# Moving the root-mean-square sums and their spread into the second weight group of two gated layers

## The chip, the core and the metric

The kernel runs on one core of a Trainium2 chip. The metric is the device time of one execution in microseconds (us), as the median of several runs. In the trace the engines are PE (TensorE, matmuls), PEld (its weight loads), DVE (VectorE), ACT (ScalarE), POOL (GpSimd) and SP (the queue that issues the loads of the weights).

## The reference, cut to what matters

Two model blocks follow one another on a sequence of 512 tokens of 1024 channels. The change touches two layers of the first block, its two gated feed-forward layers behind a root mean square (here f1 and f2):

```python
def rms_norm(x, g):
    xf = x.astype(jnp.float32)
    y = xf * lax.rsqrt(jnp.mean(xf * xf, axis=-1, keepdims=True) + NORM_EPS)
    return (y * g.astype(jnp.float32)).astype(x.dtype)

def swiglu(x, w_in, w_out):
    gate, up = jnp.split(x @ w_in, 2, axis=-1)
    return (jax.nn.silu(gate) * up) @ w_out

h = rms_norm(x, ffn1_pre_g[l])
x = x + 0.5 * rms_norm(swiglu(h, ffn1_w_in[l], ffn1_w_out[l]), ffn1_post_g[l])
```

w_in is 1024 x 5632, that is 22 tiles of 128 gate channels and 22 of up channels. The factor of the root mean square is one number per token, so it can be multiplied in behind the matmul: the gates are multiplied by it before silu and once more after silu, for the ups. Between f1 and f2 stands a mixer of attention and a state space; the second block has four more gated layers (a0, b0, a1, b1), which have a layer norm and are not touched.

## The kernel before

**Layout.** Activations are held transposed, channels on 128 partitions and the 512 tokens along the free dimension: X, and its halves Hh and Hl (a high part that the fast float format holds, and the rest). Each weight is split in the same way into whi and wlo. A product of a tile is then three matmuls of 128 x 512: hi by hi, lo by hi and hi by lo (L325 to L327, or L339, L340 and L345 where a group opens).

**Weights.** They come in units of eight 128 x 128 tiles, 512 KB each, in the order of use, and there are four slots (NS = 4). SP loads a unit once PE is done with the unit four before it. ACT copies it to whi (L792, `hi`), then DVE subtracts to get wlo (L1283, `lo`), then PE may use it. Both engines do this in program order, at most two units ahead of the tile that they stand at (AHEAD = 2, `hi_to` and `lo_to`).

**The gated layer, `ffn`.** A group is one pair of gates and the two ups that belong to it: four PSUM banks are filled by eight steps k over the input channels, 4 tiles and 12 matmuls a step, 96 in all, from four units of weights. There are 11 groups (j = 0, 2, ..., 20). I call them group 1, 2, 3 and so on, and number the layer's units from 0: group 1 uses units 0 to 3, group 2 units 4 to 7, group 3 starts with unit 8. While PE works on one group, the other engines work on the one before it, in this chain: DVE multiplies gate 0 and gate 1 by Rb (L1331, "gate in"), which empties their banks; ACT takes silu of each (L853); POOL multiplies each by Rb again (L2022); DVE multiplies by the ups (L1338), which empties the other two banks; ACT copies the product to Ah (L867) and DVE subtracts for Al (L1345). PE has eight banks, taken in turn, four of them held by the running group.

**The root mean square.** The squares are summed over channels by POOL and ACT into acc and sq. PE sums these over partitions by small matmuls (`rms_cols`, L431 and L436) beside step k = 6 of group 1; ACT takes the root (L814), DVE the reciprocal (L1305) and splits it (colr); PE spreads it over all partitions (`spread`, L446) at the end of group 1; ACT copies it to Rb (L828). So sums and spread take the banks 5 and 6 of the turn, and group 2 takes 7, 8, 1 and 2. Its third and fourth bank are those of the two gates of group 1.

**Side work.** In f1 ACT and DVE also advance a generator `s5_small`, which prepares tables for the mixer in small pieces: one piece at steps k = 2 and 5 of each group but the first, and one at the end of each pair. On ACT the pieces use Exp (L961, L964) and later Sin. Every switch between Sqrt, Exp, Silu and Sin costs an ACT_TABLE_LOAD.

Of the kernel before, what the change touches and what calls it, by code (L numbers as in the profile page):

```python
# [5 lines left out]
P = 128  # L6
T = 512
D = 1024
KD = D // P
# [171 lines left out]
def build(nc, x_d, w_d, cst_d, s5_d, att_d, msk_d, out_d):  # L181
# [52 lines left out]
        assert offset + size <= 229344, (name, offset + size)  # L234
        return nc.alloc_sbuf_tensor_at(name, list(shape), dt, offset=offset), offset

    Ah, _ = ar("Ah", [P, NF, T], F32R)
    Al, _ = ar("Al", [P, NF, T], F32R)
    Y, _ = ar("Y", [P, KD, T], F32)
    cur[0] = arena  # L240
    Qf, _ = ar("Qf", [P, 4, T], F32)
    Kf, _ = ar("Kf", [P, 4, T], F32)
# [59 lines left out]
    def tensor_program(pe):  # L302
# [153 lines left out]
                    last = name == "sq" and p_ == (1 if perm else 0)  # L456
                    col_sums(src[:, :], b, 8 * p_, (("full", (tag, "cols")),) if last else (), p_ == 1)

        def rms_mid(st, perm=False):
            def mid(k):  # L460
                if k == KD - 2:
                    rms_cols(st, perm)
                if k == KD - 1:
                    spread(0, (st, "rms"), ("spread", st))
            return mid

        def ffn(st, rms):
            for j in range(0, NF, 2):
                gemm_group((st, j), st if j == 0 else None, (("H free", st),) if j == NF - 2 else (),
                           rms_mid(st) if rms and j == 0 else None)  # L470

        def bank_squares(st, k):

# [307 lines left out]
    def scalar_program(act):  # L781
# [35 lines left out]
        def rms_mid(st, k, n=4):  # L817
            if k == KD - 2:
# [3 lines left out]
            if k == KD - 1:  # L822
# [11 lines left out]
                act.activation(X[:, k, :], X[:, k, :], ACT.Copy, scale=ALPHA).then_inc(  # L834
                    *S.done("scales", ("X scaled", st, k)))

        def ffn(st, rms, arena_free, side=None, tmp_free=()):
            for j in range(0, NF, 2):
                p = START[st] + j // 2 * 4 * KD
                for k in range(KD):  # L840
                    hi_to(p + 4 * k + 3)
                    if side and j and k in (2, 5):
                        next(side, None)
                    if j == 0 and rms:
                        rms_mid(st, k)
                if j == 2 and not rms:
                    scale_x(st)
                if not rms:
                    act.wait_ge(*S.at(("full", (st, j))))
                for i in range(2):  # L850
                    if rms:
                        act.wait_ge(*S.at(("gate in", st, j + i)))
                        act.activation(tmp[i][:, :], tmp[i][:, :], ACT.Silu).then_inc(  # L853
                            *S.done("silu", ("silu", st, j + i)))
                    else:
                        if j:
                            act.wait_ge(*S.at(("product", st, j - 2 + i)))
                        else:
                            act.wait_ge(*S.at(tmp_free + (i,)))
                        act.activation(tmp[i][:, :], bank(((st, j), i))[:, :], ACT.Silu).then_inc(  # L860
                            *S.done("silu", ("silu", st, j + i), empties=[((st, j), i)]))
                if j == 0:
                    for key in arena_free:
                        act.wait_ge(*S.at(key))
                for i in range(2):
                    act.wait_ge(*S.at(("product", st, j + i)))
                    act.activation(Ah[:, j + i, :], tmp[2 + i][:, :], ACT.Copy).then_inc(  # L867
                        *S.done("moving_hi", ("Ah", st, j + i)))
                if side:
                    next(side, None)  # L870

        def square(st, k, src):

# [376 lines left out]
            if k == 1:  # L1250
                hi(1)
        side = s5_small()
        ffn("f1", True, (), side)
# [3 lines left out]
        ffn("f2", True, (("Hl", "m1o", 7), ("full", ("glu", 3))))  # L1257
# [12 lines left out]
    def vector_program(dve):  # L1270
# [42 lines left out]
        def ffn(st, rms, arena_free, side=None):  # L1313
            for j in range(0, NF, 2):
                p = START[st] + j // 2 * 4 * KD
                for k in range(KD):
                    lo_to(p + 4 * k + 3)
                    if side and j and k in (2, 5):
                        next(side, None)
                    if rms and j == 0 and k == KD - 2:  # L1320
                        rms_recip(st, (st, "rms"))
                gate = [bank(((st, j), i))[:, :] for i in range(2)]
                up = [bank(((st, j), 2 + i))[:, :] for i in range(2)]
                dve.wait_ge(*S.at(("full", (st, j))))
                if rms:
                    if j == 0:
                        dve.wait_ge(*S.at(("Rb", st)))
                    for i in range(2):
                        if j:
                            dve.wait_ge(*S.at(("product", st, j - 2 + i)))  # L1330
                        dve.tensor_tensor(tmp[i][:, :], gate[i], Rb[:, :], MUL).then_inc(  # L1331
                            *S.done("gates", ("gate in", st, j + i), empties=[((st, j), i)]))
                for i in range(2):
                    dve.wait_ge(*S.at(("gate" if rms else "silu", st, j + i)))
                    if j:
                        dve.wait_ge(*S.at(("Al", st, j - 2 + i)))
                    keys = (("product", st, j + i),) + ((("last product", st, i),) if j == NF - 2 else ())
                    dve.tensor_tensor(tmp[2 + i][:, :], up[i], tmp[i][:, :], MUL).then_inc(  # L1338
                        *S.done("gates", *keys, empties=[((st, j), 2 + i)]))
                if j == 0:  # L1340
                    for key in arena_free:
                        dve.wait_ge(*S.at(key))
                for i in range(2):
                    dve.wait_ge(*S.at(("Ah", st, j + i)))
                    dve.tensor_tensor(Al[:, j + i, :], tmp[2 + i][:, :], f32(Ah[:, j + i, :]), SUB).then_inc(  # L1345
                        *S.done("moving_lo", ("Al", st, j + i)))
                if side:
                    next(side, None)

        def add_square(st, k, tag):  # L1350
            dve.wait_ge(*S.at(("square", st, k)))
# [622 lines left out]
            if k == 1:  # L1974
                lo(1)
        side = s5_small()
        ffn("f1", True, (), side)
# [4 lines left out]
        ffn("f2", True, (("full", ("glu", 3)),))  # L1982
# [365 lines left out]
```

## Time and profile before

| | us |
|---|---|
| median of 3 runs | 3035.84 (3031.92 to 3036.48) |
| the profiled execution's own time | 3040.53 |
| its span in the trace | 3038.7 |
| PE busy | 2953.3, 97% of the span |
| DVE busy | 1327.3, 44% |
| ACT busy | 1002.3, 33% |
| POOL busy | 403.4, 13% |
| weights, share of the 16 DMA engines | 26.4% |

Of the chain of work that ended last 93% is PE, 4% DVE, and 1% ACT. A busy share of PE counts matmuls by modelled ends that overlap their successors, so what the rows tell is the start of each matmul: at the full clock of 2.4 GHz one 128 x 512 matmul starts every 0.227 us, at 1.2 GHz every 0.43 us. Idle time in square brackets names what ended it.

### The profile page before, as it was taken

How to read it: one execution, taken by the hardware profiler on the slowest of the kernel's cores; microseconds unless marked ns; L12 is line 12 of the kernel's file. 1: busy time of each engine (PE TensorE's matmuls, PEld its weight loads, DVE VectorE, ACT ScalarE, POOL GpSimd, SP SyncE). 2: the span in 40 equal slices, each digit the busy share in tenths (PEclk: the TensorE clock that was granted, in tenths of full speed). 3: DMA queues.
4: the chain of work that ended last, by engine and by line, in shares of the span. 5: the costliest groups of instructions: out<-in, count | busy, mean ns of one | idle time of the engine just before them, and what ended most of it. 6: DMA issues, size and time to landing. Idle time of an engine off the chain costs nothing.

```text
span 3038.7 us, 32142 instructions
## 1 busy us (share of the span) xinstructions
PE 2953.3 (97%) x13432; PEld 2434.2 (80%) x13432; DVE 1327.3 (44%) x1783; ACT 1002.3 (33%) x1345; POOL 403.4 (13%) x427
## 2 busy tenths in 40 slices
PE   8999989899999999999999999999999999899998
PEld 6888876577888788888887888888888788788887
DVE  5553267645343433334655333343333465543333
ACT  4232234453232333223333332233222333342222
POOL 3110057312110000011231000100001123200010
PEclk9999989899999999999998999999999899899998
DMA  4333212122233232232212222222333221122222
GB/s 137 96 97 97 97 56 69 17 72 88 97 97 97 85 97 97 97 96 77 77 49 64 97 97 97 97 77 97 97 97 96 72 76 49 63 97 97 96 91 77
DMA packets 76016, 260.39 MB, mean 86 GB/s; under 512 B 11728, under 2 KB 11856, under 8 KB 75856
## 3 DMA queue, kind: packets, MB, share of 16 engines
q1 hardware_dynamic: 75872, 258.34, 26.4%
q8 instruction: 106, 1.74, 0.2%
q14 instruction: 38, 0.31, 0.0%
HBM read 255.03 MB, written 2.10 MB: 85 GB/s over the span
## 4 chain that ended last, share of the span: by engine, by line
PE 93%; DVE 4%; issue 1%; ACT 1%; POOL 0%; DMA 0%; SPq 0%; DVEq 0%; POOLq 0%; ACTq 0%
PE bank L325 25%; PE bank L327 25%; PE bank L326 25%; PE bank L339 2%; PE bank L340 2%; PE bank L345 2%; PE bank L436 2%; PE bank L683 2%; PE bank L446 1%; DVE Hl L1291 1%; PE bank L374 1%; PE bank L375 1%; PE bank L378 1%; PE bank L590 1%; PE bank L608 1%
## 5 line engine op out<-in xcount | busy, mean ns | idle before, releaser
L1283 DVE TENSOR_TENSOR wlo<-wraw,whi 128x1024 fp32r<-128x1024 f32 x474 | 588.1, 1253 | 832.4 <-ACT whi L792 831.7
L325 PE MATMUL bank<-Hh,whi 128*128 128x512 f32 x2320 | 911.5, 393 | 11.0 <-DVE wlo L1283 9.1
L326 PE MATMUL bank<-Hh,wlo 128*128 128x512 f32 x2320 | 906.5, 391 | 0.0
L327 PE MATMUL bank<-Hl,whi 128*128 128x512 f32 x2320 | 906.1, 391 | 0.0
L792 ACT ACTIVATE whi<-wraw 128x1024 fp32r<-128x1024 f32 x479 | 498.9, 1055 | 957.8 <-DMA wraw<-weights 957.5
L325 PEld LDWEIGHTS bank<-Hh,whi 128*128 128x128 f32 x2320 | 438.3, 189 | 106.4 <-issue 11.7
L327 PEld LDWEIGHTS bank<-Hl,whi 128*128 128x128 f32 x2320 | 437.8, 189 | 92.4
L326 PEld LDWEIGHTS bank<-Hh,wlo 128*128 128x128 f32 x2320 | 437.9, 189 | 89.3
L325 PE MATMUL bank<-Ah,whi 128*128 128x512 f32 x1056 | 411.8, 390 | 0.0
L326 PE MATMUL bank<-Ah,wlo 128*128 128x512 f32 x1056 | 410.9, 389 | 0.0
L327 PE MATMUL bank<-Al,whi 128*128 128x512 f32 x1056 | 410.8, 389 | 0.0
L327 PEld LDWEIGHTS bank<-Al,whi 128*128 128x128 f32 x1056 | 198.2, 188 | 41.3
L326 PEld LDWEIGHTS bank<-Ah,wlo 128*128 128x128 f32 x1056 | 198.3, 188 | 40.8
L325 PEld LDWEIGHTS bank<-Ah,whi 128*128 128x128 f32 x1056 | 198.3, 188 | 40.6
L1338 DVE TENSOR_TENSOR tmp<-bank,tmp 128x512 f32<-128x512 f32 x132 | 87.2, 688 | 239.6 <-ACT tmp L860 193.9
L2028 POOL TENSOR_TENSOR zsum<-Y 128x512 f32<-128x512 f32 x6 | 10.4, 1730 | 1220.6 <-DVE Y L1417 1220.6
L339 PE MATMUL bank<-Hh,whi 128*128 128x512 f32 x304 | 128.6, 423 | 24.0 <-issue 8.4
L340 PE MATMUL bank<-Hh,wlo 128*128 128x512 f32 x304 | 125.8, 414 | 0.0
L860 ACT ACTIVATE tmp<-bank 128x512 f32<-128x512 f32 x88 | 47.8, 595 | 197.3 <-PE bank L327 197.3
L2022 POOL TENSOR_TENSOR tmp<-tmp,Rb 128x512 f32<-128x512 f32 x44 | 56.0, 1295 | 413.3 <-ACT tmp L853 413.3
L867 ACT ACTIVATE Ah<-tmp 128x512 fp32r<-128x512 f32 x132 | 81.7, 632 | 62.2 <-DVE tmp L1338 62.2
L339 PEld LDWEIGHTS bank<-Hh,whi 128*128 128x128 f32 x304 | 61.3, 202 | 40.7 <-issue 18.6
(258 smaller groups left out, 2528.1 us busy)
## 6 DMA issues: line engine op xcount, KB each, us to landing
wraw<-weights SPq DMA_DIRECT2D x479, 512.0 KB, 3.4
X<-x_t SPq DMA_DIRECT2D x8, 256.0 KB, 6.9
y_t<-X SPq DMA_DIRECT2D x8, 256.0 KB, 2.0
Y<-masks SPq DMA_DIRECT2D x1, 512.0 KB, 8.5
MUb<-ssm SPq DMA_DIRECT2D x1, 256.0 KB, 7.9
tmp<-ssm SPq DMA_DIRECT2D x1, 256.0 KB, 3.9
zsum<-attention SPq DMA_DIRECT2D x1, 256.0 KB, 4.0
MUb<-attention SPq DMA_DIRECT2D x1, 256.0 KB, 4.2
```

The costliest lines, as they stand in the source:

```text
L325: pe.matmul(b, sh, mh, start=start, stop=False)
L326: pe.matmul(b, sl, mh, start=False, stop=False)
L327: signal(pe.matmul(b, sh, ml, start=False, stop=stop), keys)
L339: pe.matmul(bs[i][:, :], hi, Hh[:, 0, :], start=True, stop=False)
L340: pe.matmul(bs[i][:, :], lo, Hh[:, 0, :], start=False, stop=False)
L345: signal(pe.matmul(bs[i][:, :], hi, Hl[:, 0, :], start=False, stop=False), ends)
L436: ins = pe.matmul(b[:, col + 2 * m:col + 2 * m + 2], lhsT, ones[:, 0:2], start=False, stop=m == 3, skip_group_check=True)
L683: ins = pe.matmul(b[:, s], KS[:, h, s], QP[:, h, s], start=True, stop=True, skip_group_check=True)
L792: act.activation(whi[:, u % NS, :], wraw[:, u % NS, :], ACT.Copy).then_inc(*S.done("weights_hi", ("hi", u)))
L867: act.activation(Ah[:, j + i, :], tmp[2 + i][:, :], ACT.Copy).then_inc(*S.done("moving_hi", ("Ah", st, j + i)))
L1283: dve.tensor_tensor(wlo[:, u % NS, :], wraw[:, u % NS, :], f32(whi[:, u % NS, :]), SUB).then_inc(*S.done("weights_lo", ("lo", u)))
L1338: dve.tensor_tensor(tmp[2 + i][:, :], up[i], tmp[i][:, :], MUL).then_inc(*S.done("gates", *keys, empties=[((st, j), 2 + i)]))
```

## The change

In f1 and f2 alone (a new argument `late`):

- The column sums of PE move from step 6 of group 1 to step 2 of group 2, and the spread from the end of group 1 to the end of step 4 of group 2. Root, reciprocal and the copy to Rb move along.
- Group 1 is copied out of its four banks by ACT (`aside`, four copies of 128 x 512) into raw4, which lies over the last four tiles of Ah. The gates and ups of group 1 are then read from raw4.
- The whole pair of group 1 (`pair(0)`: gate in, silu, POOL's product, product, Ah, Al) runs on ACT and DVE at step 5 of group 2, ahead of the split of unit 9, which is done at step 6.
- The banks: group 1 takes 1 to 4, group 2 takes 5 to 8, sums and spread 1 and 2, and group 3 takes 3, 4, 5 and 6. Its third and fourth bank are those of the two gates of group 2.

```diff
+    raw4, _ = ar("raw4", [P, 4, T], F32, o_ah + (NF - 4) * T * 4)
 # PE
-                           rms_mid(st) if rms and j == 0 else None)
+                           rms_mid(st, False, 2, 4) if rms and j == 2 else None)
 # ACT
-        def ffn(st, rms, arena_free, side=None, tmp_free=()):
+        def ffn(st, rms, arena_free, side=None, tmp_free=(), late=False):
+            def aside():
+                act.wait_ge(*S.at(("full", (st, 0))))
+                for key in arena_free:
+                    act.wait_ge(*S.at(key))
+                for i in range(4):
+                    ins = act.activation(raw4[:, i, :], bank(((st, 0), i))[:, :], ACT.Copy)
+                ins.then_inc(*S.done("rows_out", ("aside", st), empties=[((st, 0), i) for i in range(4)]))
...
+            for j in range(0, NF, 2):
+                p = START[st] + j // 2 * 4 * KD
+                for k in range(KD):
+                    hi_to(p + 4 * k + 3)
+                    if side and j and k in (2, 5):
+                        next(side, None)
+                    if rms and j == (2 if late else 0):
+                        rms_mid(st, k, 4, 2 if late else KD - 2, 4 if late else KD - 1)
+                    if late and (j, k) == (2, 5):
+                        pair(0)
...
+                if late and j == 0:
+                    aside()
+                else:
+                    pair(j)
 # DVE
+            def pair(j):
+                aside = late and j == 0
+                gate = [raw4[:, i, :] if aside else bank(((st, j), i))[:, :] for i in range(2)]
+                up = [raw4[:, 2 + i, :] if aside else bank(((st, j), 2 + i))[:, :] for i in range(2)]
+                if aside:
+                    dve.wait_ge(*S.at(("aside", st)))
+                else:
+                    dve.wait_ge(*S.at(("full", (st, j))))
...
+            for j in range(0, NF, 2):
+                p = START[st] + j // 2 * 4 * KD
+                for k in range(KD):
+                    lo_to(p + 4 * k + 3)
+                    if side and j and k in (2, 5):
+                        next(side, None)
+                    if rms and (j, k) == ((2, 3) if late else (0, KD - 2)):
+                        rms_recip(st, (st, "rms"))
+                    if late and (j, k) == (2, 5):
+                        pair(0)
+                if not (late and j == 0):
+                    pair(j)
```

On ACT in f1, from the root of the mean square on. Before (sp_80 are the tables of the side work, weights0 to weights3 the slots):

```order
L814 ACTIVATE small<-bank,epsc 128x4 [waits matmul]
L828 ACTIVATE Rb<-bank 128x512 [waits matmul]
L853 ACT_TABLE_LOAD
L853 ACTIVATE tmp_67<-tmp_67 128x512 [waits gates]
L853 ACTIVATE tmp_68<-tmp_68 128x512 [waits gates]
L867 ACTIVATE Ah<-tmp_69 128x512 [waits gates]
L867 ACTIVATE Ah<-tmp_70 128x512 [waits gates]
L792 ACTIVATE whi<-wraw 128x1024 [waits weights2]
L792 ACTIVATE whi<-wraw 128x1024 [waits weights3]
L961 ACT_TABLE_LOAD
L961 ACTIVATE sp_80<-cst 128x16
L792 ACTIVATE whi<-wraw 128x1024 [waits weights0]
```

And after the change, where the line L793 is the split of a unit, L829 the copy to Rb, L855 silu, L869 the copy to Ah, and L980 and L983 are the Exps of the side work:

```order
L793 ACTIVATE whi<-wraw 128x1024 [waits weights0]
L829 ACTIVATE Rb<-bank 128x512 [waits matmul]
L980 ACT_TABLE_LOAD
L980 ACTIVATE sp_80<-cst 128x16
L855 ACT_TABLE_LOAD
L855 ACTIVATE tmp_67<-tmp_67 128x512 [waits gates]
L855 ACTIVATE tmp_68<-tmp_68 128x512 [waits gates]
L869 ACTIVATE Ah<-tmp_69 128x512 [waits gates]
L869 ACTIVATE Ah<-tmp_70 128x512 [waits gates]
L983 ACT_TABLE_LOAD
L983 ACTIVATE sp_80<-sp_80 128x16 [waits s5_dve]
L793 ACTIVATE whi<-wraw 128x1024 [waits weights1]
```

The Exp pieces now stand on both sides of the pair of group 1, and the split of unit 9 (weights1) behind all of it; the splits of units 6 and 7 (weights2, weights3) have moved ahead of the root.

On DVE in f1, the pair of group 1 and what follows. Before:

```order
L1331 TENSOR_TENSOR tmp_67<-bank,Rb 128x512 [waits scales,matmul]
L1331 TENSOR_TENSOR tmp_68<-bank,Rb 128x512
L1338 TENSOR_TENSOR tmp_69<-bank,tmp_67 128x512 [waits pool_gates]
L1338 TENSOR_TENSOR tmp_70<-bank,tmp_68 128x512 [waits pool_gates]
L1345 TENSOR_TENSOR Al<-tmp_69,Ah 128x512 [waits moving_hi]
L1345 TENSOR_TENSOR Al<-tmp_70,Ah 128x512 [waits moving_hi]
L1497 CAST msk<-Y 128x1024 [waits masks]
L1283 TENSOR_TENSOR wlo<-wraw,whi 128x1024 [waits weights_hi] x3
```

After, down to the first gate of group 2:

```order
L1349 TENSOR_TENSOR tmp_67<-raw_85,Rb 128x512 [waits scales,rows_out]
L1349 TENSOR_TENSOR tmp_68<-raw_85,Rb 128x512
L1356 TENSOR_TENSOR tmp_69<-raw_85,tmp_67 128x512 [waits pool_gates]
L1356 TENSOR_TENSOR tmp_70<-raw_85,tmp_68 128x512 [waits pool_gates]
L1363 TENSOR_TENSOR Al<-tmp_69,Ah 128x512 [waits moving_hi]
L1363 TENSOR_TENSOR Al<-tmp_70,Ah 128x512 [waits moving_hi]
L1516 TENSOR_TENSOR sp_80<-sp_80,cst 128x16 [waits s5_dve,s5_act]
L1516 TENSOR_TENSOR sp_80<-sp_80,cst 128x16 [waits s5_dve]
L1520 TENSOR_SCALAR sp_80<-sp_80 128x16 [waits s5_dve] x2
L1302 TENSOR_TENSOR wlo<-wraw,whi 128x1024 [waits weights_hi]
L1349 TENSOR_TENSOR tmp_67<-bank,Rb 128x512 [waits gates,matmul]
```

Between the pair of group 1 and the first gate of group 2 there now stands, besides a piece of side work, one wlo (unit 9), which waits for ACT; before there stood four.

On ACT in f2 after the change, which has no side work:

```order
L815 ACTIVATE small<-bank,epsc 128x4 [waits matmul,columns]
L793 ACTIVATE whi<-wraw 128x1024 [waits weights0]
L829 ACTIVATE Rb<-bank 128x512 [waits matmul,rows]
L855 ACT_TABLE_LOAD
L855 ACTIVATE tmp_67<-tmp_67 128x512 [waits gates]
L855 ACTIVATE tmp_68<-tmp_68 128x512 [waits gates]
L869 ACTIVATE Ah<-tmp_69 128x512 [waits gates,matmul,moving_lo]
L869 ACTIVATE Ah<-tmp_70 128x512 [waits gates]
L793 ACTIVATE whi<-wraw 128x1024 [waits weights1]
```

Here the split of unit 9 follows the last copy to Ah at once.

## Rows read from the trace of the kernel before

**Rows 1.** The page: span, and busy time of PE.

```profile
span 3038.7 us, 32142 instructions
PE 2953.3 (97%) x13432; PEld 2434.2 (80%) x13432; DVE 1327.3 (44%) x1783; ACT 1002.3 (33%) x1345; POOL 403.4 (13%) x427
```

**Rows 2.** The waits of PE: us in total, times, longest us.

```profile
PE bank L339 <- DVE tmp L1331: 1.1, 2, 0.6
```

**Rows 3.** Timeline of PE in f1 (start us, us): group 2 opens, group 3 opens.

```profile
40.33 0.45 PE L339 MATMUL bank<-Hh,whi 128*128 128x512 f32 x1
...
41.98 0.50 PE L339 MATMUL bank<-Hh,whi 128*128 128x512 f32 x1 [0.52 <-DVE tmp L1331]
...
43.15 1.09 PE L345 MATMUL bank<-Hl,whi 128*128 128x512 f32 x4
...
63.13 0.39 PE L339 MATMUL bank<-Hh,whi 128*128 128x512 f32 x1
```

**Rows 4.** Timeline of ACT in f1: Rb, pair of group 1, first Exp, a split.

```profile
40.53 0.60 ACT L828 ACTIVATE Rb<-bank 128x512 f32<-128x512 f32 x1 [3.43 <-PE bank L446]
41.15 1.28 ACT L853 ACT_TABLE_LOAD   x1
42.44 1.15 ACT L853 ACTIVATE tmp<-tmp 128x512 f32<-128x512 f32 x2
...
46.46 0.63 ACT L867 ACTIVATE Ah<-tmp 128x512 fp32r<-128x512 f32 x1 [0.62 <-DVE tmp L1338]
...
49.02 1.28 ACT L961 ACT_TABLE_LOAD   x1
50.31 0.22 ACT L961 ACTIVATE sp<-cst 128x16 f32<-128x16 f32 x1
...
55.93 1.06 ACT L792 ACTIVATE whi<-wraw 128x1024 fp32r<-128x1024 f32 x1 [2.60 <-DMA wraw<-weights]
```

**Rows 5.** Timeline of DVE in f1: gates, second product, a split, gates of group 2.

```profile
41.24 1.29 DVE L1331 TENSOR_TENSOR tmp<-bank,Rb 128x512 f32<-128x512 f32 x2 [3.52 <-ACT Rb L828]
...
45.73 0.69 DVE L1338 TENSOR_TENSOR tmp<-bank,tmp 128x512 f32<-128x512 f32 x1 [0.56 <-POOL tmp L2022]
...
57.02 1.23 DVE L1283 TENSOR_TENSOR wlo<-wraw,whi 128x1024 fp32r<-128x1024 f32 x1 [3.31 <-ACT whi L792]
63.33 1.29 DVE L1331 TENSOR_TENSOR tmp<-bank,Rb 128x512 f32<-128x512 f32 x2 [5.08 <-PE bank L327]
```

**Rows 6.** Timeline of POOL in f1: both products of the pair of group 1.

```profile
43.15 2.55 POOL L2022 TENSOR_TENSOR tmp<-tmp,Rb 128x512 f32<-128x512 f32 x2 [15.32 <-ACT tmp L853]
```

**Rows 7.** Timeline of f2, all engines, where group 2 opens.

```profile
703.32 0.45 PE L339 MATMUL bank<-Hh,whi 128*128 128x512 f32 x1
...
704.28 1.29 DVE L1331 TENSOR_TENSOR tmp<-bank,Rb 128x512 f32<-128x512 f32 x2 [3.52 <-ACT Rb L828]
...
705.02 0.50 PE L339 MATMUL bank<-Hh,whi 128*128 128x512 f32 x1 [0.58 <-DVE tmp L1331]
...
706.19 1.09 PE L345 MATMUL bank<-Hl,whi 128*128 128x512 f32 x4
...
710.04 1.99 ACT L792 ACTIVATE whi<-wraw 128x1024 fp32r<-128x1024 f32 x2
```

**Rows 8.** Timeline of PE: restarts after idle stretches of 3.66, 1.91 and 3.00 us.

```profile
24.86 0.47 PE L325 MATMUL bank<-Hh,whi 128*128 128x512 f32 x1 [3.66 <-DVE wlo L1283]
...
29.27 0.39 PE L325 MATMUL bank<-Hh,whi 128*128 128x512 f32 x1
...
694.90 0.47 PE L325 MATMUL bank<-Hh,whi 128*128 128x512 f32 x1 [1.91 <-DVE wlo L1283]
695.20 0.39 PE L326 MATMUL bank<-Hh,wlo 128*128 128x512 f32 x1
...
2627.68 0.77 PE L325 MATMUL bank<-Hh,whi 128*128 128x512 f32 x1 [3.00 <-DVE wlo L1283]
...
2633.71 0.40 PE L327 MATMUL bank<-Hl,whi 128*128 128x512 f32 x1
```

**Rows 9.** Stretches: us, busy by engine (x instructions), then granted clock of PE, DMA.

```profile
25.00:30.00 5.00, 5.00 (x16) 3.95 (x17) 5.00 (x3) 2.07 (x2) 2.75 (x2) 0.66 0.00 0
```

More of the change, by code:

```diff
@@ L457, in rms_cols, with rms_mid @@
                     col_sums(src[:, :], b, 8 * p_, (("full", (tag, "cols")),) if last else (), p_ == 1)
-        def rms_mid(st, perm=False):
+        def rms_mid(st, perm=False, first=KD - 2, second=KD - 1):
             def mid(k):
-                if k == KD - 2:
+                if k == first:
                     rms_cols(st, perm)
-                if k == KD - 1:
+                if k == second:
                     spread(0, (st, "rms"), ("spread", st))
@@ L815, in rms_root, with rms_mid @@
                            bias=epsc[:, 0:1]).then_inc(*S.done("roots", ("root", tag), empties=[(tag, "cols")]))
-        def rms_mid(st, k, n=4):
-            if k == KD - 2:
+        def rms_mid(st, k, n=4, first=KD - 2, second=KD - 1):
+            if k == first:
                 if st == "f2":
@@ L821, in rms_mid @@
                 rms_root(st, n)
-            if k == KD - 1:
+            if k == second:
                 if st == "m1":
@@ L835, in scale_x @@
                     *S.done("scales", ("X scaled", st, k)))
-        def ffn(st, rms, arena_free, side=None, tmp_free=()):
[L838 to L847, printed above, removed]
+        def ffn(st, rms, arena_free, side=None, tmp_free=(), late=False):
[7 more added lines that the diff above has]
+            def pair(j):
                 if not rms:
@@ L870, in ffn @@
                     next(side, None)
+            for j in range(0, NF, 2):
[8 more added lines that the diff above has]
+                        pair(0)
+                if j == 2 and not rms:
+                    scale_x(st)
+                if late and j == 0:
+                    aside()
+                else:
+                    pair(j)
         def square(st, k, src):
@@ L1252, in scalar_program @@
         side = s5_small()
-        ffn("f1", True, (), side)
+        ffn("f1", True, (), side, (), True)
         out_rms("f1", NF, row_ends("f1"), ["masks kept"], "f1")
@@ L1256, in scalar_program @@
         mixer_1()
-        ffn("f2", True, (("Hl", "m1o", 7), ("full", ("glu", 3))))
+        ffn("f2", True, (("Hl", "m1o", 7), ("full", ("glu", 3))), None, (), True)
         out_rms("f2", NF, row_ends("f2"), [("post a", "m1o")], "f2")
@@ L1311, in rms_recip, with ffn, pair @@
             spread_cols(rcol[:, 0:4], 0, use, tag)
[L1313 to L1324, printed above, removed]
+        def ffn(st, rms, arena_free, side=None, late=False):
+            def pair(j):
+                aside = late and j == 0
[5 more added lines that the diff above has]
+                    dve.wait_ge(*S.at(("full", (st, j))))
                 if rms:
@@ L1331, in ffn @@
                         dve.tensor_tensor(tmp[i][:, :], gate[i], Rb[:, :], MUL).then_inc(
-                            *S.done("gates", ("gate in", st, j + i), empties=[((st, j), i)]))
+                            *S.done("gates", ("gate in", st, j + i), empties=[] if aside else [((st, j), i)]))
                 for i in range(2):
@@ L1338, in ffn @@
                     dve.tensor_tensor(tmp[2 + i][:, :], up[i], tmp[i][:, :], MUL).then_inc(
-                        *S.done("gates", *keys, empties=[((st, j), 2 + i)]))
+                        *S.done("gates", *keys, empties=[] if aside else [((st, j), 2 + i)]))
                 if j == 0:
@@ L1976, in vector_program @@
         side = s5_small()
-        ffn("f1", True, (), side)
+        ffn("f1", True, (), side, True)
         out_rms("f1", row_ends("f1"))
@@ L1981, in vector_program @@
         mixer_1()
-        ffn("f2", True, (("full", ("glu", 3)),))
+        ffn("f2", True, (("full", ("glu", 3)),), None, True)
         out_rms("f2", row_ends("f2"))
```

2 lines of the change are left out of this document (1 added, 1 removed).

## The prediction

> **What bounds the kernel now.** The page comes first: PE is busy for 97% of the span [rows 1], so only what makes PE wait, or what PE itself does more or less of, can move the end. Then the list of PE's waits, for the wait that this change aims at: the opening of group 2 waits for the first "gate in" of DVE, 1.1 us in two places [rows 2], one in f1 and one in f2. The rest comes from the timelines around those two places. In f1 group 2 starts at 40.33; its third bank is that of gate 0, and gate 0 can only be multiplied when Rb is there, which comes from the spread that PE itself ended at 40.33. So the matmul that needs the bank starts at 41.98 [rows 3].
>
> Two measures are needed throughout. The pace: from 43.15 to 63.13 stand 88 matmuls [rows 3], 19.98 us, 0.227 us each; a step k of 12 is 2.72 us, four are 0.91. And a time origin: I call E the moment at which the spread ends and the next matmul starts. Before, E is 40.33 in f1 and 703.32 in f2 [rows 3, 7].
>
> **What the wait costs today.** From the start of group 2 to its L345 there are eight matmuls, 1.82 us at the pace. The first one behind a spread takes 0.06 more (its partner starts 0.29 instead of 0.23 later); I keep that on both sides. In f1 L345 starts at 43.15, that is 2.82 after E, and would start 1.88 after it: 0.94 lost. In f2 it is 706.19 - 703.32 = 2.87: 0.99 lost [rows 3, 7]. Of each, 0.26 is not the wait proper but the slower restart at the two waiting matmuls: from 41.98 to 43.15 are 1.17 us for four matmuls, 0.26 over the pace. Removing both waits in full gives 1.93 us. That is the most that this change can gain, 0.06% of the time.
>
> **What moves at no cost.** The column sums and the spread are the same instructions on PE, in another group. The four copies into raw4 are new on ACT. The nearest row for one is the copy of a bank to Rb, 0.60 us [rows 4], so 2.4 us at most. They run when group 1 is full, at the start of group 2, where ACT otherwise has nothing but the splits of units 6 and 7; PE reaches unit 6 four steps later, 10.9 us. That hides copies and splits (2.4 + 2 x 1.06), and even at double the price it would. Their last one also frees the bank for the column sums, two to three steps (8.2 us) later. If a copy cost nothing nothing would be gained either. Reading raw4 instead of a bank changes an operand's place; the DVE rows of that size all stand at 0.6 to 0.7, and I take 0 with 0.1 either way. The mask CAST of DVE moves ahead, into its idle time. Rb is no longer late for group 2.
>
> **What takes the wait's place.** Group 3 now takes the banks of the gates of group 2 as its third and fourth. In the kernel before, group 3 found its banks free. So PE waits for the "gate in" of group 2, and what matters is when DVE gets to it. The order on DVE is: pair of group 1, (side work in f1), wlo of unit 9, gate in of group 2. The wlo waits for ACT's whi of unit 9, and on ACT that stands behind the last copy to Ah of the pair of group 1. The whole chain of group 1 hence lies between E and the gates, and E is now the end of the spread at step 4, with only steps 5, 6 and 7 left. PE wants the third bank at E + 0.06 + 3 x 2.72 + 0.91 = E + 9.14.
>
> *f1, step by step from E.* Rb starts at +0.20 and its table load at +0.82 (40.53 and 41.15 less 40.33) [rows 4]. What stands next on ACT is not silu but the Exp of the side work: a load of 1.28 and its 0.01 of distance, Exp 0.22, then again a load for Silu of 1.29. Silu starts at 0.82 + 1.29 + 0.23 + 1.29 = +3.63, where it was +2.11 before (42.44). "Gate in" ran at +0.9 and is no limit. From silu to POOL 0.71 (43.15 less 42.44) [rows 4, 6], from there to the second product on DVE 2.58 (45.73) [rows 5], to the second copy to Ah 0.73 (46.46), and 0.63 for it: +8.28. Then the second Exp: load 1.29 and 0.23, so +9.80. It waits for a product of the side work on DVE, which follows the last Al and is there by about +9.2. The split of unit 9: 1.06, and DVE starts 1.09 after ACT did (55.93 and 57.02) [rows 4, 5], +10.89. wlo takes 1.2: +12.09. Gate in, and the matmul behind it, 0.74 after that (41.24 to 41.98): +12.83. PE wanted it at +9.14: 3.7 late, and with the restart of 0.26 3.95 us lost, against 0.94 before: **+3.0 us**. That unit 9 has landed by then is safe: its slot is free after step 3 of group 2, which ended in the trace at 43.15 + 0.91 + 3 x 2.72 = 52.2, and its split began at 55.93, 3.7 later. Now step 3 ends a step and a spread before E, some 3.5 us, so the unit is there at about +0.2.
>
> *f2.* No side work. Gate in of group 1 starts at +0.96, the split behind the last Ah 5.76 after that (710.04 less 704.28) [rows 7], +6.72. wlo starts 1.09 later, takes 1.2, gate in and matmul 0.74: +9.75. Late by 0.61, with the restart 0.87, against 0.99 before: **-0.1 us**. So here one wait is swapped for an almost equal one.
>
> **The clock.** The wait of 3.7 us in f1 is also long enough to matter for PE's clock. After 3.00 us idle in a busy stretch PE restarts at the 1.2 GHz level: from 2627.68 to 2633.71 are 13 matmuls in 6.03 us, where the pace gives 2.95, so 3.1 us lost, 3.0 without the restart. After 3.66 us idle at 24.86 the granted clock of the next stretch was 0.66 [rows 9], and 12 matmuls took 4.41 instead of 2.72 (to 29.27), 1.6 lost besides the restart. After 1.91 us at 694.90 the next matmul followed at 0.30 and nothing was slow [rows 8]. The new wait is as long as the two that brought the low clock. I take the middle, **+2.3 us**, with 1.6 and 3.0 as its usual ends and 0 as the outer one. The waits in f2, 0.6 us, cost no clock.
>
> **Sum.** 3.0 - 0.1 + 2.3 = +5.2 us. Against the profiled execution's own time that is 3040.53 to 3045.7. The median of the runs shown is 3035.84, 4.7 below the profiled one, and the difference carries over: 3041.0. Everything behind f1 is paced by PE, and I see nothing that would take the loss up again.
>
> **A rule of the Trainium skill against the rows.** In f1 three table loads now lie on the path, and the one before was hidden beside "gate in". Rows 4 show what follows a load: loads at 41.15 and 49.02 last 1.28, and the next ACTIVATE starts 0.01 us later. The Trainium skill's "ScalarE: Activation LUTs", section "What ACT_TABLE_LOAD costs", gives about 1283 ns for the load and about 1380 ns more for a drain with every switch. By that the chain of f1 would be longer by 3 x 1.38 = 4.1 us, an estimate from that page, and the sum +9.3. The rows show the load alone, and I go by them.
>
> **The rivals.**
>
> *The clock stays up* after the wait: then +2.9 us, 3038.7. For it: the busy stretch before is long and the restart at 24.86 ran its first matmuls at full pace. Against it: 2627.68 also had a busy stretch before it. 15%.
>
> *The gain comes as meant*: if DVE gets to the gates of group 2 in time, that is if the chain from E to gate in is under 9.1 us, both waits vanish: -1.9, 3033.9. It would take ACT doing the Exps or the split of unit 9 elsewhere than the order shows. For it: the sums and durations of f2 come within 0.6 of that point, so it could hold there. Against it: f1 is 3.7 off. With f1 on time by some overlap I don't see: 12%.
>
> *Slower than can be called no change.* The mechanism is the same wait in f1, longer and with a longer slow clock. It decides from +6.1, that is when the slow stretch costs more than 3.2 us, 16 matmuls at 0.43 instead of 0.227, or when the wait grows by about 1 us, for which the side piece on DVE (dependent small operations, each waiting for the one before) or Exp's wait for it would have to be a us longer than I have it. Price +6.1 to +8.5. For it: 13 matmuls were slow at 2627.68, and that idle stretch was shorter than this one. 25%, 3042 to 3044.3.
>
> *A drain behind each load*, as worked out above from +1.38 each: +9.3, 3045.1, 3%, since no load in the rows has one.
>
> **How the numbers follow.** The forecast has 45%: 3041.0. The range shall hold 8 in 10: forecast with its clock term of 1.6 to 3.0, the clock that stays up, most of the slower case, and the 2 us or so by which medians of such runs differ: 3034 to 3045. A measurement can tell 0.2%, 6.1 us, from no change. Forecast, steady clock and the full gain all lie within it; the slower case and the drain lie beyond, and the forecast's own upper end comes close, as the steady clock lies well inside. Faster 0.02 (the full gain with a measurement that errs by 4 us), same 0.70, slower 0.28.
>
> **What would show it.** In the profile of the changed kernel: the wait of L339 for DVE's gate in is gone at the opening of group 2 and stands at that of group 3, 3.7 us in f1 and 0.6 in f2; two Exp loads around the silu of group 1 on ACT; behind the wait in f1 ten or more matmuls at 0.43. I would be wrong if the wait in f1 is under 2 us (then the order of ACT's work is not what holds DVE), if no matmul behind it is slow, or if a new wait shows at a place that I did not name, for a unit of weights above all.

## The result, and the profile after

| | before | after |
|---|---|---|
| median of 18 runs, us | 3035.87 (3031.22 to 3042.13) | 3040.29 (3036.23 to 3046.26) |
| profiled span, us | 3038.7 | 3036.0 |
| PE's wait for the gates in, us in all | 1.1 | 4.6 |

The ratio of the runs is 1.0018 with a 95% interval of 1.0012 to 1.0025: 5.5 us slower by the ratio, 4.4 by the medians. The ratio itself is below the 0.2% named in the prediction (the upper end of its interval is not), and the interval leaves no doubt about the sign.

One profiled execution can't show this by its span: the changed one happens to be 2.7 us shorter. So the loss is read from the distance between matmuls at the place of the change. The waits of PE after the change, as in [rows 2]:

```profile
span 3036.0 us, 32153 instructions
PE bank L340 <- DVE tmp L1349: 4.6, 2, 3.8
```

The opening of group 3 in f1 and, behind the dots, what comes after; it answers to [rows 3]. Lines of the matmuls are one higher than before, the spread is L447, the root L815, Rb L829:

```profile
53.56 1.00 PE L447 MATMUL bank<-identr,colr 128*128 128x128 f32 x8
...
62.62 0.39 PE L340 MATMUL bank<-Hh,whi 128*128 128x512 f32 x1
...
67.50 0.79 PE L340 MATMUL bank<-Hh,whi 128*128 128x512 f32 x1 [3.81 <-DVE tmp L1349]
...
69.37 1.76 PE L346 MATMUL bank<-Hl,whi 128*128 128x512 f32 x4
...
71.43 0.40 PE L328 MATMUL bank<-Hl,whi 128*128 128x512 f32 x1
```

Group 2 now opens without a wait. Group 3 opens at 62.62, its third bank is wanted four matmuls later at 63.53 and used at 67.50: 3.97 us late. ACT in that stretch, answering to [rows 4]:

```profile
54.60 0.60 ACT L829 ACTIVATE Rb<-bank 128x512 f32<-128x512 f32 x1 [5.20 <-PE bank L447]
55.22 1.28 ACT L980 ACT_TABLE_LOAD   x1
56.51 0.22 ACT L980 ACTIVATE sp<-cst 128x16 f32<-128x16 f32 x1
56.74 1.28 ACT L855 ACT_TABLE_LOAD   x1
58.04 1.15 ACT L855 ACTIVATE tmp<-tmp 128x512 f32<-128x512 f32 x2
61.88 1.24 ACT L869 ACTIVATE Ah<-tmp 128x512 fp32r<-128x512 f32 x2 [2.68 <-DVE tmp L1356]
63.13 1.28 ACT L983 ACT_TABLE_LOAD   x1
64.42 0.22 ACT L983 ACTIVATE sp<-sp 128x16 f32<-128x16 f32 x1
64.55 1.04 ACT L793 ACTIVATE whi<-wraw 128x1024 fp32r<-128x1024 f32 x1
```

And DVE, answering to [rows 5]: both products, Al, the low part of unit 9, the gates of group 2.

```profile
60.08 2.36 DVE L1356 TENSOR_TENSOR tmp<-raw,tmp 128x512 f32<-128x512 f32 x2 [3.48 <-POOL tmp L2053]
62.54 1.29 DVE L1363 TENSOR_TENSOR Al<-tmp,Ah 128x512 fp32r<-128x512 f32 x2
...
65.62 1.23 DVE L1302 TENSOR_TENSOR wlo<-wraw,whi 128x1024 fp32r<-128x1024 f32 x1 [1.07 <-ACT whi L793]
66.76 1.28 DVE L1349 TENSOR_TENSOR tmp<-bank,Rb 128x512 f32<-128x512 f32 x2
```

One reads down the two: Rb at 54.60, two table loads before silu starts at 58.04, a third one behind Ah, then the split of unit 9 at 64.55, its low part at 65.62, and only then, at 66.76, the gate that PE has wanted since 63.53. In f2, which has no Exps, the same opening (the first row is the spread):

```profile
717.58 1.00 PE L447 MATMUL bank<-identr,colr 128*128 128x128 f32 x8
...
726.64 0.39 PE L340 MATMUL bank<-Hh,whi 128*128 128x512 f32 x1
...
728.53 0.50 PE L340 MATMUL bank<-Hh,whi 128*128 128x512 f32 x1 [0.81 <-DVE tmp L1349]
...
729.69 1.09 PE L346 MATMUL bank<-Hl,whi 128*128 128x512 f32 x4
```

**The loss at a place.** For every kernel below I take one number for each layer: the time from the opening of the group that waits to the L346 of the group after it, less 1.82 us for the eight matmuls and less 21.76, the distance of two openings in an undisturbed stretch. It holds the wait, the restart and the slow matmuls. For the kernels that wait at group 2, it holds the 0.06 us that a spread costs the matmul behind it as well, and I take this off, as it is paid in every kernel. Before: 0.97 in f1 and 1.02 in f2, 0.03 more than the prediction's measure, which ended at the opening itself. After: from 62.62 to 91.85 are 29.23 us, 5.65 lost in f1, and 1.25 in f2. Net +4.68 and +0.23, +4.9 us in all.

**Why the span says otherwise.** The matmuls of the last layer stand 2.70 us earlier than before, while those of a1 stand 1.24 later. The difference arises at two waits around the last mixer, in code that is the same in both kernels. The first is a wait of 2.23 us for sums of POOL, which ends at 2603.11 before and at 2604.34 after the change. Behind it the granted clock was 0.50, the 1.2 GHz level, in the kernel before and 1.00 in the changed one (the third number from the end of the rows that begin with a stretch), which makes 2.7 us. The first two rows are the kernel before, the other two the changed one:

```profile
2603.11 1.87 PE L436 MATMUL bank<-ones,zsum 128*128 128x2 f32 x8 [2.23 <-POOL zsum L2028]
2603.00:2608.00 5.00, 4.89 (x16) 4.22 (x17) 0.23 (x2) 0.00 (x0) 0.05 (x1) 0.50 0.01 2
...
2604.34 1.05 PE L437 MATMUL bank<-ones,zsum 128*128 128x2 f32 x8 [2.23 <-POOL zsum L2059]
2604.00:2609.00 5.00, 4.58 (x23) 3.63 (x23) 1.59 (x5) 0.00 (x0) 0.91 (x2) 1.00 0.02 6
```

The second is the wait of 3.0 us before 2627.68 in [rows 8], where the clock was low at once. After the change the same wait ends so:

```profile
2626.20 0.47 PE L326 MATMUL bank<-Hh,whi 128*128 128x512 f32 x1 [2.98 <-DVE wlo L1302]
2626.51 0.40 PE L327 MATMUL bank<-Hh,wlo 128*128 128x512 f32 x1
...
2627.44 0.63 PE L328 MATMUL bank<-Hl,whi 128*128 128x512 f32 x1
```

The first five matmuls start at full pace here, and only then are they slow: 1.15 us less than before. The start of the program differs as well: from the L346 of group 1 of f1 to the opening of group 2 it is 26.8 us here and 23.1 in e5 and e8 below, with the same work. These are differences between executions. They are as large as the effect, so the verdict comes from many runs and the mechanism from the rows at the place.

The second wait is a measure of how large they get, since all eleven kernels of this document have it, with the same code and 2.98 to 3.02 us long. The 30 matmuls behind it took longer than at the pace by 0.12 us in e2, by 1.5 to 1.7 in seven kernels and by 2.9 in three. In e2 the clock never fell:

```profile
2623.34 0.47 PE L326 MATMUL bank<-Hh,whi 128*128 128x512 f32 x1 [3.02 <-DVE wlo L1302]
2623.40:2625.40 2.00, 2.00 (x9) 1.65 (x10) 1.09 (x2) 1.57 (x2) 1.30 (x1) 1.00 0.00 0
```

### The profile page after: what moved, and what is told of

The parts are those of the page before. It is cut to its first block, busy times and chain, and to the rows that moved or that the text cites. A ratio compares the mean times of both kernels' runs of the same rounds, so it can differ in the third digit from the quotient of the medians.

```text
span 3036.0 us, 32153 instructions
## 1 busy us (share of the span) xinstructions
PE 2946.5 (97%) x13432; PEld 2431.1 (80%) x13432; DVE 1326.4 (44%) x1783; ACT 1007.4 (33%) x1354; POOL 403.4 (13%) x427
## 4 chain that ended last, share of the span: by engine, by line
PE 91%; DVE 5%; ACT 2%; issue 2%; POOL 1%; DMA 0%; SPq 0%; POOLq 0%; DVEq 0%; ACTq 0%
PE bank L326 24%; PE bank L328 24%; PE bank L327 24%; PE bank L340 2%; PE bank L341 2%; PE bank L346 2%; PE bank L437 2%; PE bank L684 2%; PE bank L447 1%; DVE Hl L1310 1%; PE bank L375 1%; PE bank L376 1%; PE bank L379 1%; PE bank L609 1%; PE bank L591 1%
## 5 line engine op out<-in xcount | busy, mean ns | idle before, releaser
L793 ACT ACTIVATE whi<-wraw 128x1024 fp32r<-128x1024 f32 x479 | 499.1, 1055 | 951.8 <-DMA wraw<-weights 951.6
L869 ACT ACTIVATE Ah<-tmp 128x512 fp32r<-128x512 f32 x132 | 81.5, 632 | 63.2 <-DVE tmp L1356 63.2
```

The source lines that it names most:

```text
L793: act.activation(whi[:, u % NS, :], wraw[:, u % NS, :], ACT.Copy).then_inc(*S.done("weights_hi", ("hi", u)))
```

## The experiments

The kernel before ran beside each of them: 30 runs beside e1, e2, e3 and e8, 33 beside e4 to e7 and 13 beside e9. Each changed kernel below ran 10 to 12 times, e8 only 5. Losses are those defined above, f1 and f2, from the profiled execution. The net of e7 also holds 1.96 us that it gains at another place of f2.

| kernel | wait f1, f2 (us, as the trace lists it) | lost f1, f2 | net against before | ratio to before (95%) |
|---|---|---|---|---|
| before | 0.52, 0.58 | 0.97, 1.02 | 0 | 1 |
| changed | 3.81, 0.81 | 5.65, 1.25 | +4.91 | 1.0018 (1.0012 to 1.0025) |
| e1, f1 only | 3.81, 0.58 | 6.80, 1.00 | +5.81 | 1.0013 (1.0004 to 1.0022) |
| e2, f2 only | 0.53, 0.81 | 0.95, 1.25 | +0.21 | 1.0000 (0.9990 to 1.0010) |
| e3, no Exps beside the pair | 0.75, 0.81 | 1.20, 1.25 | +0.46 | 1.0000 (0.9989 to 1.0010) |
| e8, Exps in f2 too | 3.81, 3.83 | 5.84, 6.70 | +10.55 | 1.0031 (1.0019 to 1.0043) |
| e4, unit 9 behind the gates | 1.51, none | 1.94, 0.30 | +0.25 | 1.0002 (0.9993 to 1.0010) |
| e5, e3 and e4 | none, none | 0.32, 0.32 | -1.35 | 0.9999 (0.9990 to 1.0008) |
| e6, e3 and a step earlier | none, none | 0.31, 0.31 | -1.37 | 0.9997 (0.9988 to 1.0005) |
| e7, before with the sums a step earlier | none, none | 0.30, 0.32 | -3.33 | 0.9994 (0.9985 to 1.0003) |
| e9, ups left in their banks | 3.40, 0.40 | 6.51, 0.83 | +5.35 | 1.0005 (0.9994 to 1.0015) |

**e1 and e2: which layer.** The argument `late` is given to one of the two calls only.

```diff
-                           rms_mid(st, False, 2, 4) if rms and j == 2 else None)
+                           (rms_mid(st, False, 2, 4) if j == 2 else None) if rms and st == "f1" else rms_mid(st) if rms and j == 0 else None)
-        ffn("f2", True, (("Hl", "m1o", 7), ("full", ("glu", 3))), None, (), True)
+        ffn("f2", True, (("Hl", "m1o", 7), ("full", ("glu", 3))))
```

> Only f1 has the change, f2 is as before. If the wait of f1 with its slow matmuls is the loss, group 3 of f1 opens with a wait of 3.8 us for the gate in, PE loses 5.6 us there where it lost 0.94, and the median is 4 to 5 us above the kernel before. If the loss lay in f2 or in both alike, it is 2.5 us or less above.

> Only f2 has the change. By the same theory f2 swaps one wait (0.58 us) for another (0.8 us), no matmul is slow, and the median is within 0.5 us of the kernel before, as far as that can be told. If f2 carries half of the loss, it is 2 to 2.5 us above.

Measured: medians 3041.10 and 3036.36, with 3035.67 for the kernel before. With f1 alone the wait of 3.81 is there and the whole loss with it, f2 alone can't be told from before. The opening of group 3 with f1 alone:

```profile
65.47 0.79 PE L340 MATMUL bank<-Hh,whi 128*128 128x512 f32 x1 [3.81 <-DVE tmp L1349]
...
67.34 1.91 PE L346 MATMUL bank<-Hl,whi 128*128 128x512 f32 x4
```

The wait repeats to 0.01 us. The clock behind it does not: 6.80 lost instead of 5.65.

**e3 and e8: the Exps.** e3 holds back the side work at step 5 of group 2 and behind the pair of group 1, on ACT and DVE alike, and does two more pieces in group 3:

```diff
-                    if side and j and k in (2, 5):
+                    if side and (k in ((2,) if j == 2 else (1, 2, 3, 5) if j == 4 else (2, 5)) if late else k in (2, 5)) and j:
...
-                if side:
+                if side and not (late and j == 0):
                     next(side, None)
```

e8 does the opposite and gives f2 what f1 has, an Exp of one column with its load on either side of the pair:

```diff
                     if late and (j, k) == (2, 5):
+                        if not side:
+                            table(ACT.Exp)
                         pair(0)
+                        if not side:
+                            table(ACT.Exp)
```

> The whole change, but in f1 the two pieces of side work beside the pair of group 1 (with their Exps) are done in group 3. Theory: the chain from the spread to the gates of group 2 loses two table loads and two Exps, 3.0 us; the wait of f1 falls from 3.8 to 0.8 us, no matmul behind it is slow, and the sum is 4.4 us below the changed kernel, about 0.5 us above the kernel before. Rival, the split of unit 9 alone holds DVE up: then the wait stays above 3 us. Rival, each load costs a drain of 1.4 us besides: then the chain would lose 5.8 us and the wait be gone.

> The whole change, and in f2 an Exp of one column with its table load on either side of the pair of group 1, where f1 has its side work. Theory: two loads and Exps of 1.5 us each lengthen the chain, the wait of f2 goes from 0.8 to 3.8 us, 4 to 8 matmuls behind it run at 0.43 us, and the kernel is 4.4 us slower than the changed one. Rival, what f1 pays for is the side work on DVE and not the loads: then f2 stays at 0.8 us. Rival, a drain behind each load: a wait of 6.6 us.

Measured: 3037.87 for e3, 3045.46 for e8. (A median of some ten runs wanders: that of e3 lies 2.2 us above the kernel before, its ratio is 1.0000.) The openings of group 3, f1 of e3 first:

```profile
63.92 0.50 PE L340 MATMUL bank<-Hh,whi 128*128 128x512 f32 x1 [0.75 <-DVE tmp L1349]
```

then f1 and f2 of e8:

```profile
64.00 0.50 PE L340 MATMUL bank<-Hh,whi 128*128 128x512 f32 x1 [3.81 <-DVE tmp L1353]
...
731.72 0.80 PE L340 MATMUL bank<-Hh,whi 128*128 128x512 f32 x1 [3.83 <-DVE tmp L1353]
```

Taking two loads and two Exps away shortens the wait by 3.06 us, adding them where none were lengthens it by 3.02. That is 1.5 for a load with its small Exp, what the rows gave. No drain shows; with the 1.38 us of the Trainium skill's "ScalarE: Activation LUTs", section "What ACT_TABLE_LOAD costs", it would have been 2.9, an estimate from that page. And with the wait at 0.75 no matmul behind it is slow. The runs agree: the interval of e3 lies below that of the changed kernel. The rival that the side work on DVE is what costs falls with e8, which adds nothing on DVE.

**e4 and e5: the split of unit 9.** DVE stops at unit 8 in group 2 and does the low part of unit 9 behind the two gates in; e5 has the edit of e3 besides.

```diff
                         dve.tensor_tensor(tmp[i][:, :], gate[i], Rb[:, :], MUL).then_inc(
                             *S.done("gates", ("gate in", st, j + i), empties=[] if aside else [((st, j), i)]))
+                if late and j == 2:
+                    lo_to(START[st] + 2 // 2 * 4 * KD + 4 * (KD - 1) + 3)
...
-                    lo_to(p + 4 * k + 3)
+                    if not (late and j == 2 and k > 5):
+                        lo_to(p + 4 * k + 3)
```

> The whole change, but DVE does the low part of unit 9 behind the gates in of group 2 instead of ahead of them; so the gates no longer wait for ACT's split of that unit. Theory: in f2 the pair of group 1 ends on DVE at 8.1 us after the spread and group 2 is full at 8.4, so its wait (0.8 us) is gone but for 0.05; in f1 DVE is free after the side work at 10.1, the gate is in at 10.9 where PE wants it at 9.1: a wait of 1.7 us instead of 3.8, with no or few slow matmuls. 4 to 5 us below the changed kernel, which is within 0.5 us of the kernel before. Rival, the pair of group 1 itself is what is late: then both waits stay.

> Both: side work of f1 in group 3, and the low part of unit 9 behind the gates in. Theory: both waits are gone but for some 0.1 us with a restart of 0.1 to 0.26, and nothing else is late: PE loses 0.15 to 0.4 us in each layer where the kernel before lost 0.94 and 0.99. 1.2 to 1.6 us below the kernel before, hardly to be told in the median. Rival, something that these waits hid is late next (a unit of weights): then no gain in the trace.

Measured: 3035.15 and 3034.54, with 3035.12 for before. The third bank of group 3, in f1 and in f2 of e4, then the same of e5:

```profile
65.03 0.50 PE L340 MATMUL bank<-Hh,whi 128*128 128x512 f32 x1 [1.51 <-DVE tmp L1349]
...
724.05 0.50 PE L340 MATMUL bank<-Hh,whi 128*128 128x512 f32 x1
```

```profile
60.15 0.19 PEld L340 LDWEIGHTS bank<-Hh,whi 128*128 128x128 f32 x1 [0.30 <-DVE tmp L1349]
60.15 0.50 PE L340 MATMUL bank<-Hh,whi 128*128 128x512 f32 x1
...
722.52 0.50 PE L340 MATMUL bank<-Hh,whi 128*128 128x512 f32 x1
```

The wait of f1 falls to 1.5 us and no matmul is slow, the one of f2 is gone. With both edits none is left. The 0.50 us matmuls without a bracket are the restart: the load of their weights (PEld) waited 0.30 us for the gate in, so it wasn't done ahead; two of them cost 0.3 in a layer. Both the split of unit 9 and the Exps held the gates of f1 up: without the one the wait is 2.30 us shorter, without the other 3.06, without both it is gone. In f2 it was the split alone. The interval of e4, too, lies below that of the changed kernel. The gain of 1.35 us that is left is below what the medians can tell.

**e6: everything a step earlier.** Sums at step 1, spread at step 3, pair of group 1 at step 4, with the side work as in e3.

```diff
-                           rms_mid(st, False, 2, 4) if rms and j == 2 else None)
+                           rms_mid(st, False, 1, 3) if rms and j == 2 else None)
...
-                    if rms and (j, k) == ((2, 3) if late else (0, KD - 2)):
+                    if rms and (j, k) == ((2, 2) if late else (0, KD - 2)):
...
-                    if late and (j, k) == (2, 5):
+                    if late and (j, k) == (2, 4):
```

> Side work of f1 in group 3, unit 9 as in the change, and sums, spread and pair of group 1 one step (2.72 us) earlier in group 2: at steps 1, 3 and 4. Theory: PE wants the third bank at 11.8 us after the spread, the chain has it there at 10.1: no wait. The same 1.2 to 1.9 us below the kernel before as with both other edits. Rival, the bank of the sums isn't free that early or unit 8 is split too late: a new wait at step 1 or at the opening of group 3.

Measured: 3035.46. No wait at either place, none at step 1, and losses equal to those of e5 by another way. The bank of the sums was free in time.

**e7: the kernel before, with sums and spread one step earlier in group 1.** No copy, no move to group 2:

```diff
-                if k == KD - 2:
+                if k == (5 if st in ("f1", "f2") else KD - 2):
                     rms_cols(st, perm)
-                if k == KD - 1:
+                if k == (6 if st in ("f1", "f2") else KD - 1):
                     spread(0, (st, "rms"), ("spread", st))
```

The same steps are changed on ACT and DVE.

> The kernel before, with nothing moved to group 2: in f1 and f2 the sums stand at step 5 of group 1 instead of 6 and the spread at step 6 instead of 7. Theory: Rb is there before group 1 ends, so group 2 waits only for the gate in after a full group, 0.1 us with restarts up to 0.35 in all instead of 0.94 and 0.99; and in f2 the sums fall into the 1.9 us in which PE waits for a unit's low part before step 6, which hides them. 3 us below the kernel before, the best of all. Rival, the sums wait for POOL's acc at step 5 in f2 and DVE's reciprocal delays the low parts of the units: then the wait grows instead and nothing is gained in f2.

Measured: 3033.14, the lowest median of all; 0.9994 with an interval of 0.9985 to 1.0003, so it can't be called faster than before by the runs, but it is faster than the changed kernel, whose interval lies above it. The third bank of group 2 in f1, then the sums in f2 with the step behind them:

```profile
41.60 0.50 PE L339 MATMUL bank<-Hh,whi 128*128 128x512 f32 x1
...
692.43 1.03 PE L436 MATMUL bank<-ones,acc 128*128 128x2 f32 x8
693.32 1.03 PE L436 MATMUL bank<-ones,sq 128*128 128x2 f32 x8
694.35 0.47 PE L325 MATMUL bank<-Hh,whi 128*128 128x512 f32 x1
```

Rb comes before group 1 ends, and the bank is there after four matmuls. In f2 the sums stand where the kernel before waited 1.91 us for a unit's low part [rows 8], and step 6 then follows with no wait: from the first L345 of f2, at 677.98, to the opening of group 2 at 703.32 [rows 7] there were 25.34 us, now 23.44, and that now holds the 0.06 behind the spread too, so 1.96 less. With -0.67 and -0.70 at the openings that is 3.33 us.

**e9: the long product.** Only the two gates are copied; the ups stay in their banks until the product of DVE.

```diff
-                for i in range(4):
+                for i in range(2):
                     ins = act.activation(raw4[:, i, :], bank(((st, 0), i))[:, :], ACT.Copy)
...
-                up = [raw4[:, 2 + i, :] if aside else bank(((st, j), 2 + i))[:, :] for i in range(2)]
+                up = [bank(((st, j), 2 + i))[:, :] for i in range(2)]
```

> The whole change, but only the two gates of group 1 are copied to raw4; the ups stay in their banks, where DVE's product reads them. In the changed kernel the first product from raw4 takes 1.77 us while POOL works on the second gate, and ends after POOL does. Theory: DVE waits for POOL when both of its inputs lie in SBUF; with one input in a bank the product takes 0.69, the second product starts 0.4 us earlier, and both waits of the changed kernel are 0.4 us shorter (0.4 in f2, 3.4 in f1), 0.8 us in all. Rival, the long product is late for another reason (its semaphore, the order of the queue): then it stays at 1.7 us and the waits at 0.81 and 3.81.

Measured: 3039.42, with 3037.24 for before. The product of DVE by its operands, in the changed kernel (ns, least, median, most):

```profile
L1356 DVE TENSOR_TENSOR tmp<-bank,tmp x128: 678/691/693, 69.5 to 2893.6; 128x512 f32<-128x512 f32 x128
L1356 DVE TENSOR_TENSOR tmp<-raw,tmp x4: 676/1218/1765, 60.1 to 724.3; 128x512 f32<-128x512 f32 x4
```

The two gates in (DVE) and the two products of POOL in f1 of the changed kernel:

```profile
55.31 1.29 DVE L1349 TENSOR_TENSOR tmp<-raw,Rb 128x512 f32<-128x512 f32 x2 [4.65 <-ACT Rb L829]
58.75 2.55 POOL L2053 TENSOR_TENSOR tmp<-tmp,Rb 128x512 f32<-128x512 f32 x2 [30.45 <-ACT tmp L855]
```

The two products of DVE in f1 of e9, then both waits of PE:

```profile
58.36 0.69 DVE L1356 TENSOR_TENSOR tmp<-bank,tmp 128x512 f32<-128x512 f32 x1 [3.48 <-POOL tmp L2053]
59.62 0.69 DVE L1356 TENSOR_TENSOR tmp<-bank,tmp 128x512 f32<-128x512 f32 x1 [0.57 <-POOL tmp L2053]
```

```profile
65.36 0.80 PE L340 MATMUL bank<-Hh,whi 128*128 128x512 f32 x1 [3.40 <-DVE tmp L1349]
...
729.59 0.50 PE L340 MATMUL bank<-Hh,whi 128*128 128x512 f32 x1 [0.40 <-DVE tmp L1349]
```

The long product is gone and both waits are 0.41 us shorter. So the operand's place was the reason: with both inputs in SBUF a product on DVE that starts beside POOL's product (60.08, POOL until 61.30) ends only after it. Two inputs in SBUF alone cost nothing: both gates in, at 55.31, have them too and took 1.29 together, with POOL idle. The loss in f1 is none the less 6.51, above the changed kernel's 5.65, because the clock was low for longer in this execution. The runs (+1.5 us by the ratio, up to +4.6 by its interval) can't tell it from the 4.1 us that the shorter waits would give.

## Why the prediction was right, point by point

**The way and the size.** 3041.0 was forecast, 3040.3 measured; the loss was forecast as 5.2 us and is 5.5 by the ratio. The path held step by step. That the sum fits so closely is in part luck: in the profiled execution the waits cost 0.6 us more than forecast and the slow clock 0.9 less, and the medians of the kernel before, 3035.12 to 3037.24 in four sets of runs, differ by more than the 0.7 us between forecast and result.

**The wait that goes, the one that comes.** The opening of group 2 has no wait, that of group 3 has it, in both layers. e1 and e2 place the loss in f1.

**The chain in f1.** With the spread's end at 54.40 (53.56 and 0.84, as the spread before, from its start to the next matmul): Rb +0.20, first load +0.82, silu +3.64 (forecast +3.63), POOL +4.35 (+4.34), split of unit 9 +10.15 (+9.80), low part +11.22 (+10.89), the matmul +13.10 (+12.83). The forecast wait of 3.7 is 3.97 by the same measure.

**The term that was mis-sized** is the product from raw4. The prediction took "an operand's place" at 0 with 0.1 either way, since all DVE rows of that size stood at 0.6 to 0.7. None of those ran beside POOL with both inputs in SBUF. It cost 0.4 us in each layer (e9), which is the whole difference of the f2 forecast (-0.1 against +0.23) and that of the f1 chain, less 0.1 from steps taken a little long. The Trainium skill's "SBUF — State Buffer", section "SBUF: two separate sides", states that a DVE op with two SBUF inputs and a GpSimd op that reads SBUF shut each other out for a whole instruction; 1.77 us against 0.69 agrees, and the page would have given the missing term.

**The clock.** Forecast 2.3 with 1.6 and 3.0 as ends. For the waits of 3.4 to 3.8 us, the loss less the lateness and the restart of 0.26 was: changed kernel 5.65 - 3.97 - 0.26 = 1.4; f1 of e1 2.6; f1 and f2 of e8 1.6 and 2.5; f1 of e9 2.7. The mean is 2.2; the changed kernel's own profile lies just below the range that was given as usual. The upper end was set a little too high by a miscount: from 2627.68 to 2633.71 [rows 8] are 14 matmuls and not 13, so 2.9 us were lost there and not 3.1. Nor is the length of the wait what sets the cost, as the prediction has it: the same wait of 3.0 us cost between 0.1 and 2.9 us (above), and in f1 of e1 a wait of only 1.88 us in group 1 brought the low clock, where the one of 1.91 in [rows 8] brought none:

```profile
23.27 0.59 PE L326 MATMUL bank<-Hh,whi 128*128 128x512 f32 x1 [1.88 <-DVE wlo L1302]
23.30:25.30 2.00, 2.00 (x5) 1.58 (x6) 2.00 (x2) 0.30 (x1) 1.86 (x2) 0.54 0.39 154
```

What decides it stays open. In the changed kernel the stretch behind the wait shows the granted clock at one half (the third number from the end; behind it the DMA's share and GB/s):

```profile
68.00:70.00 2.00, 2.00 (x6) 1.52 (x5) 0.55 (x2) 0.70 (x2) 1.81 (x2) 0.50 0.00 0
```

"Ten or more matmuls at 0.43" was too much: 8 were slow here.

**What moves at no cost.** The four copies took 2.07 us at the start of group 2 and nothing waited for them. No unit of weights was late at a new place; unit 9 had landed.

**The rivals.** *The clock stays up*: no, in five of five waits of 3.4 us and more at these openings. But it did once in eleven behind the wait of 3.0 us (e2), so it was right to give it a chance. *The gain as meant*: no, and e5 and e6 show what it takes: the Exps and unit 9 off the path, or a step more of time with the Exps off it. *Slower than can be told*: the wait was longer by 0.3, and in e1's trace the clock brings the loss to +5.81, near the 6.1 from which this rival counts. The upper end of the measured interval, 7.6 us, lies beyond it. It was the right neighbour to have given 25%. *A drain*: no, by e3 and e8.

**The ceiling** of 1.93 us was for removing both waits in full. e5 and e6 reach 1.4: the third and fourth bank still come just in time, and the restart of 0.3 stays. e7 goes past the ceiling because it also uses another wait, which the prediction didn't look for: it asked what the change gains, not where else in the layer the sums could stand.

## What to carry to other kernels

A stage that is moved later to take one wait away gives up its slack to the next consumer: count the whole chain from the moved step to the next thing that PE wants, with everything that stands between on each engine, side work and table loads too. Look first for a smaller move in the other direction: one step earlier, into an idle stretch that PE has anyway, gave more here, in the trace, than the copy, the new buffer and the second group; the runs can't tell that gain from nothing. And where an effect is a few us in 3000, read it as a distance between matmuls at the place, since two executions of the same code differ by as much elsewhere.

## What the hardware showed that I had not expected

- A wait of PE of 3.8 us repeats to 0.02 us between executions, but what the clock costs behind it goes from 1.4 to 2.6 us, and behind one and the same wait of 3.0 us, in eleven traces, from 0.1 to 2.9. In some cases (f1 of e8, 2626.20 of the changed kernel) the first matmuls start at full pace and then turn slow, in others they are slow at once. The waits of 0.4 to 1.5 us at these openings brought no slow matmul, but one of 1.88 us in f1 of e1 did.
- A product on DVE from two SBUF operands took 1.77 us instead of 0.69 while POOL was at a product of its own, and 0.69 again when one operand was left in a PSUM bank.
- A matmul whose wait ends just before it is due costs a restart of some 0.15 us, though the list of waits shows nothing for PE, only 0.30 us for its weight load: 0.3 us in each layer of e5, e6 and e7.
